# Loops for the gathers and for part of the slots, side work moved ahead

## The reference

```
hx: 272 tokens x 1024, normalized
scores of 8 heads x 2 halves against 128 keys each; the 16 best pairs per head
expert = 128 * index_a + index_b          # 8 heads x 16 = 128 experts per token, of 16384
gate   = softmax over the 16 of a head
act    = gelu(hx . peer_u[expert])        # one dot of 1024 per token and expert
y      = sum over the 128 of gate * act * peer_v[expert]
```

## Time and profile before

| | us |
|---|---|
| median of 3 runs | 2488.28 (2478.59 to 2488.97) |
| the profiled execution | 2487.36, span 2485.6 |
| PE busy | 1982.1 (80%) |
| DVE busy | 1413.1 (57%) |
| POOL busy | 1027.1 (41%), 528 + 528 gathers |
| ACT busy | 576.7 (23%) |

### The profile page before, as it was taken

How to read it: one execution, slowest core, us unless ns; L and a number is a source line. 1 busy time by engine, 2 the same in 40 slices (tenths; PEclk the granted TensorE clock), 3 DMA queues, 4 the chain that set the end, 5 groups by cost and what they waited for, 6 DMA issues and landing times.

```text
span 2485.6 us, 21257 instructions
## 1 busy us (share of the span) xinstructions
PE 1982.1 (80%) x6918; PEld 1101.4 (44%) x6918; DVE 1413.1 (57%) x3068; ACT 576.7 (23%) x1204; POOL 1027.1 (41%) x1063
## 2 busy tenths in 40 slices
PE   6756767767898789768877887688877799897998
PEld 3641222222333335423344463243322297676996
DVE  0138788755344554694455447855555455555884
ACT  1111100100112431011134211111100134453663
POOL 0025656766444454464444545656666400000000
PEclk9888989999998889999988899999999899998999
DMA  3257989999889789989966899999999744353653
GB/s 146 85 168 309 371 314 367 369 368 356 320 301 345 272 285 393 348 305 357 396 235 234 329 385 346 343 370 409 396 364 368 284 144 154 111 153 103 187 182 122
DMA packets 194843, 707.96 MB, mean 285 GB/s; under 512 B 21784, under 2 KB 23072, under 8 KB 194480
## 3 DMA queue, kind: packets, MB, share of 16 engines
q0 software_dynamic: 152064, 553.72, 59.6%
q1 hardware_dynamic: 40960, 150.65, 17.9%
q10 hardware_dynamic: 1712, 2.24, 0.3%
HBM read 704.81 MB, written 1.06 MB: 284 GB/s over the span
## 4 chain that ended last, share of the span: by engine, by line
PE 54%; DVE 17%; issue 10%; DMA 7%; POOL 6%; ACT 3%; another core or an unknown queue 1%; ACTq 0%; SPq 0%; DVEq 0%; POOLq 0%
PE ps L494 22%; PE ps L652 15%; DMA a<-in_peer_u,eidx 7%; PE ps L411 5%; PE ps L426 5%; DVE a L1435 4%; POOL a L349 3%; POOL a L344 3%; DVE diag L1444 1%; DVE a L1369 1%; PE ps L444 1%; PE ps L397 1%; PE ps L598 1%; DVE a L1375 1%
## 5 line engine op out<-in xcount | busy, mean ns | idle before, releaser
L494 PE MATMUL ps<-a,diag 128*128 128x512 f32 (+1 forms) x2112 | 1091.9, 657 | 356.2 <-DVE diag L1444 237.2
L494 PEld LDWEIGHTS ps<-a,diag 128*128 128x128 f32 (+1 forms) x2112 | 402.9, 203 | 994.2 <-issue 623.0
L1435 DVE SCALAR_TENSOR_TENSOR a<-a,ps 128x1024 f32<-128x1024 f32 x512 | 622.3, 1216 | 347.3 <-DMA a<-in_peer_u,eidx 289.3
L344 POOL DMA_INDIRECT a<-in_peer_u,eidx x528 | 522.5, 990 | 636.7 <-DVE a L1435 303.4
L349 POOL DMA_INDIRECT a<-in_peer_v,eidx x528 | 503.8, 954 | 303.3 <-issue 133.3
L652 PE MATMUL ps<-a_r 128*128 128x256 f32 (+1 forms) x1648 | 393.8, 332 | 19.9 <-DVE a_r L1583 7.3
L932 ACT ACTIVATE gel<-dots 128x1 f32<-128x1 f32 x528 | 101.1, 201 | 1076.6 <-DVE a L1435 637.9
L652 PEld LDWEIGHTS ps<-a_r 128*128 128x128 f32 x1648 | 279.6, 192 | 52.3 <-DVE a_r L1583 8.1
L1577 DVE TENSOR_TENSOR ring_r<-wring,a_r 128x1024 fp32r<-128x1024 f32 x142 | 173.3, 1222 | 139.8 <-ACT a_r L1091 139.7
L1444 DVE TENSOR_SCALAR diag<-cstc,gel,a 128x128 f32<-128x128 f32 (+1 forms) x528 | 186.1, 354 | 104.0 <-issue 38.9
L1091 ACT ACTIVATE a_r<-wring 128x1024 fp32r<-128x1024 f32 x142 | 149.4, 1053 | 82.3 <-PE ps L652 82.2
(11 more groups left out here) (218 smaller groups left out, 1299.1 us busy)
## 6 DMA issues: line engine op xcount, KB each, us to landing
wring<-in_units SPq DMA_DIRECT2D x270, 512.0 KB
a<-in_peer_u,eidx POOLq DMA_INDIRECT x528
a<-in_peer_v,eidx POOLq DMA_INDIRECT x528
cs2c<-in_cs SPq DMA_DIRECT2D x1, 1792.0 KB
a<-in_poolm SPq DMA_DIRECT2D x1, 1632.0 KB, 9.2
h<-in_xin SPq DMA_DIRECT2D x2, 512.0 KB, 4.2
bcF<-in_bc_rows SPq DMA_DIRECT2D x2, 512.0 KB, 9.3
a<-in_mem SPq DMA_DIRECT2D x1, 1024.0 KB, 4.9
```

Source lines behind the costliest of these rows:

```text
L344: g.indirect_dma_start(ug[:, n % NU, :], None, peer_u, bass.IndirectOffsetOnAxis(ap=eidx[:, t, k:k + 1], axis=0))\
L494: last = nc.tensor.matmul(ps[0:P, 6 + j, :], diag[:, k % 4, 0:P], vg[:, k % NV, j * 512:(j + 1) * 512], start=False, stop=False)
L1435: v.scalar_tensor_tensor(ug[:, n % NU, :], ug[:, n % NU, :], 1.0, hnm if t == 2 else ps2(4), ALU.mult, ALU.mult, accum_out=dots[:, k % 8:k ...
```

## The change

- POOL's gathers of the four big tiles are in loops (`g.Fori`) of 32 slots a turn. In a loop the number n is a register. Before every 16 slots POOL copies 16 columns of `eidx` into a new tile `ixc` of two halves and waits for the copy. The waits for `dot` and `vsum` stand apart from the gathers, as each is followed by an increment of a new semaphore (`u_go`, `v_go`) that nothing waits for; the two are built as one instruction. The 16 meta slots and the first tile's two halves stay as they were in order: the first tile has two loops of two turns.
- PE's sums of the first tile are a loop of four turns (`sums_loop`).
- DVE and ACT do slots 96 to 127 of the first tile in a loop of one turn, PE, ACT and DVE slots 64 to 127 of the last tile in a loop of two turns (`slots_loop`, `gelu_loop`, `sums_loop`). Buffer numbers come from the slot's place in the turn, the values waited for from registers.
- In `SIDE`, `flip` goes from 56 to 54 and `first` from 112 to 60; a new entry `end` = 64 is where the loops begin.

```diff
...
                                           "in_z", "br", "out", "up", "down"]
-SIDE = dict(mem=3, memT=6, mem_k=9, mem_v=22, trev=36, n2=42, n2T=46, x=49, flip=56, first=112)
+SIDE = dict(mem=3, memT=6, mem_k=9, mem_v=22, trev=36, n2=42, n2T=46, x=49, flip=54, first=60, end=64)
...
         ti = sb("ti", [128, 256], u32)
         bp = sb("bp", [128, 128], u32)
         pab = sb("pab", [128, 2, 128], u32)
+        ixc = sb("ixc", [128, 2, 16], u32)
         eidx = sb("eidx", [128, 3, 128], u32)
         dots = sb("dots", [128, 8])
         gel = sb("gel", [128, 8])
...
             g.memset(ss[:, :], 1.0).then_inc(S("zeroed"), 1)
             g.memset(hsum[:, :], 1.0).then_inc(S("zeroed"), 1)
-            def slot(t, k, n):
-                if n >= NU:
-                    g.wait_ge(S("dot"), n + 1 - NU)
-                g.indirect_dma_start(ug[:, n % NU, :], None, peer_u,
-                                     bass.IndirectOffsetOnAxis(ap=eidx[:, t, k:k + 1], axis=0))\
-                    .then_inc(S(f"u{n % NU}"), 16)
-                if n >= NV:
-                    g.wait_ge(S("vsum"), n + 1 - NV)
-                g.indirect_dma_start(vg[:, n % NV, :], None, peer_v,
-                                     bass.IndirectOffsetOnAxis(ap=eidx[:, t, k:k + 1], axis=0))\
-                    .then_inc(S(f"v{n % NV}"), 16)
+            n_idx = [0]
+            def indices(half, src):
+                g.tensor_copy(ixc[:, half, :], src).then_inc(S("ixc"), 1)
+            def slot(l, k, n, half, col):
+                if not isinstance(n, int) or n >= NU:
+                    g.wait_ge(S("dot"), n + (1 - NU))
+                    g.sem_inc(S("u_go"), 1)
+                g.indirect_dma_start(ug[:, k % NU, :], None, peer_u,
+                                     bass.IndirectOffsetOnAxis(ap=ixc[:, half, col:col + 1], axis=0))\
+                    .then_inc(S(f"u{k % NU}"), 16)
+                if not isinstance(n, int) or n >= NV:
+                    g.wait_ge(S("vsum"), n + (1 - NV))
+                    g.sem_inc(S("v_go"), 1)
+                g.indirect_dma_start(vg[:, k % NV, :], None, peer_v,
+                                     bass.IndirectOffsetOnAxis(ap=ixc[:, half, col:col + 1], axis=0))\
+                    .then_inc(S(f"v{k % NV}"), 16)
             for l in range(2):
                 for t, base in gathers(l):
                     g.wait_ge(S("eidx"), tk_number(l, t))
-                    for k in range(16 if t == 2 else SLOTS):
-                        if (l, t, k) == (0, 0, SLOTS // 2):
-                            g.wait_ge(S("eidx"), tk_number(0, 0, 1))
-                        slot(t, k, base + k)
+                    if t == 2:
+                        indices(1, eidx[:, t, 0:16])
+                        n_idx[0] += 1
+                        g.wait_ge(S("ixc"), n_idx[0])
+                        for k in range(16):
+                            slot(l, k, base + k, 1, k)
+                        continue
+                    done = n_idx[0]
+                    turns = SLOTS // GB
+                    for part, (i0, i1) in enumerate([(0, turns // 2), (turns // 2, turns)] if (l, t) == (0, 0)
+                                                    else [(0, turns)]):
+                        if part:
+                            g.wait_ge(S("eidx"), tk_number(l, t, part))
+                        with g.Fori(i0, i1) as i:
+                            for half in range(2):
+                                indices(half, eidx[:, t, ds(i * GB + 16 * half, 16)])
+                                g.wait_ge(S("ixc"), 2 * i + (done + half + 1))
+                                for kk in range(16):
+                                    k = 16 * half + kk
+                                    slot(l, k, GB * i + (base + k), half, kk)
+                    n_idx[0] += 2 * (SLOTS // GB)
         @block.tensor
         def _(pe):
...
                 last.then_inc(S("y_pe"), 1)
                 owe("y", m, 6, 7)
+            def sums_loop(base, start=0):
+                with pe.Fori(start // GB, SLOTS // GB) as i:
+                    for k in range(GB):
+                        sums_slot(128, k, GB * i + (base + k), 16 * (GB // NV) * i + 16 * ((base + k) // NV + 1))
             def beside(base):
                 return Beside(lambda k: sums_slot(128, k, base + k, 16 * ((base + k) // NV + 1)), LAG)
...
                 sums_slot(META, k, m_base + k, 16 * ((m_base + k) // NV + 1))
             sums_end(2, 1)
             sums_begin(128)
-            first = beside(a_base)
-            first.to(SLOTS + LAG)
+            sums_loop(a_base)
             sums_end(0, 2)
             def front(i, bg):
...
                                         start=True, stop=True)
             last.then_inc(S("flip_pe"), 1)
             owe("bias", 1, 0, 1, 2, 3)
-            bg.to(SLOTS + LAG)
+            bg.to(SIDE["end"] + LAG)
+            sums_loop(b_base, SIDE["end"])
             sums_end(1, 5)
             owe("dot", 16 + 4 * SLOTS, 4, 5)
...
                 nc.scalar.activation(gel[:, k % 8:k % 8 + 1], dots[:, k % 8:k % 8 + 1], ACT.Gelu)\
                     .then_inc(S("gelu"), 1)
+            def gelu_loop(base, start=0):
+                with act.Fori(start // GB, SLOTS // GB) as i:
+                    for k in range(GB):
+                        gelu(k, GB * i + (base + k))
             def beside(base):
                 return Beside(lambda k: gelu(k, base + k))
...
             gate_exps(0, 0, 1)
             first.to(TOPK_B)
             gate_exps(0, 1)
-            first.to(SLOTS)
+            first.to(STRAIGHT)
+            gelu_loop(a_base, STRAIGHT)
             x_row(1)
             y_out(0, 2)
...
             bg.to(SIDE["first"])
             w_high(SPLIT0)
             w_high(SPLIT0 + 1)
-            bg.to(SLOTS)
+            bg.to(SIDE["end"])
+            gelu_loop(b_base, SIDE["end"])
             y_out(1, 5)
...
                 link(v.reciprocal(gs[:, h0:h0 + H], gm[:, h0:h0 + H]))
                 link(v.tensor_tensor(G3, G3, gs[:, h0:h0 + H].unsqueeze(2).to_broadcast([128, H, 16]), ALU.mult))
-            def dot(t, k, n):
-                dve.wait_ge(S(f"u{n % NU}"), 16 * (n // NU + 1))
-                if t < 2 and k == 0:
+            def dot(t, k, n, ufill=None):
+                dve.wait_ge(S(f"u{k % NU}"), 16 * (n // NU + 1) if ufill is None else ufill)
+                if t < 2 and isinstance(n, int) and n % SLOTS == 16:
                     dve.wait_ge(S("x_row"), (n - 16) // SLOTS + 1)
-                v.scalar_tensor_tensor(ug[:, n % NU, :], ug[:, n % NU, :], 1.0, hnm if t == 2 else ps2(4),
+                v.scalar_tensor_tensor(ug[:, k % NU, :], ug[:, k % NU, :], 1.0, hnm if t == 2 else ps2(4),
                                        ALU.mult, ALU.mult, accum_out=dots[:, k % 8:k % 8 + 1]).then_inc(S("dot"), 1)
             def coef(t, k, n, gate):
                 unit_mat, W = (cc("sel", 16), 16) if t == 2 else (ident, 128)
                 dve.wait_ge(S("gelu"), n + 1)
-                if n >= 4:
+                if not isinstance(n, int) or n >= 4:
                     dve.wait_ge(S("vsum"), n - 3)
                 v.tensor_scalar(diag[:, k % 4, 0:W], unit_mat, gel[:, k % 8:k % 8 + 1], gate,
                                 ALU.mult, ALU.mult).then_inc(S("diag"), 1)
...
             def flush(t, base, n):
                 for k in (n - 2, n - 1):
                     coef(t, k, base + k, gates[t][:, k:k + 1])
+            def slots_loop(t, base, start=0):
+                with dve.Fori(start // GB, SLOTS // GB) as i:
+                    for k in range(GB):
+                        dot(t, k, GB * i + (base + k), 16 * (GB // NU) * i + 16 * ((base + k) // NU + 1))
+                        if k >= 2:
+                            coef(t, k - 2, GB * i + (base + k - 2), gates[t][:, ds(GB * i + (k - 2), 1)])
+                    for k in (GB - 2, GB - 1):
+                        coef(t, k, GB * i + (base + k), gates[t][:, ds(GB * i + k, 1)])
             norm("f0", [0, 1, 2], 3, gain=bcF[:, :])
...
             topk(0, 0, lambda n: bg.to(min(TOPK_A, TOPK_A * n / HALF_GATE_AT)), part=1)
             dve.wait_ge(S("sc0_ev"), 3)
             topk(0, 1, lambda n: bg.to(min(STRAIGHT, TOPK_A + (TOPK_B - TOPK_A) * n / GATE_AT)))
-            bg.to(SLOTS)
-            flush(0, a_base, SLOTS)
+            bg.to(STRAIGHT)
+            flush(0, a_base, STRAIGHT)
+            slots_loop(0, a_base, STRAIGHT)
             def heads_norm(tag, tiles):
...
             bg.to(SIDE["first"] + 1)
             w_low(SPLIT0)
             w_low(SPLIT0 + 1)
-            bg.to(SLOTS)
-            flush(1, b_base, SLOTS)
+            bg.to(SIDE["end"])
+            flush(1, b_base, SIDE["end"])
+            slots_loop(1, b_base, SIDE["end"])
             dve.wait_ge(S("vsum"), 16 + 4 * SLOTS)
```

## The result

The changed kernel takes 2502.47 us (median of 5 runs, 2500.34 to 2510.94), the kernel before 2485.21 us (5 runs, the three shown above and two more). The ratio is 1.0081, 95% interval 1.0056 to 1.0106: 20 us slower, by the medians 17. It was measured twice more in the experiments, 1.0082 (1.0063 to 1.0102) and 1.0080 (1.0064 to 1.0096).

A forecast was written before the change was run, and what follows sets the result against it. Row arrival by DMA was taken to bound the first and last tile, with POOL hardly faster. POOL's terms 25 + 19 + 21 = 65 us, times 0.27, gave 18 us: 2487.4 + 18 = 2505 us, range 2484 to 2562.

The forecast's parts named there:

- The bound: In the first and last tile slots come as fast as rows arrive; POOL, hardly faster, has 0.08 us margin per slot.
- Term 1: On POOL, 33 index copies for the loops at 0.75 us each, between 0.4 and 1.15: 25 us.
- Term 2: On POOL, separate waits ahead of gathers, charged only where POOL waits: 234 gathers at 0.08 us, 19 us.
- Term 3: On POOL, 11 jumps back in the loops, each charged an instruction fetch of 1.9 us: 21 us.
- Terms 4 and 5: Loops of PE, DVE and ACT (0 to 3 us) and the last tile's moved side work (below 2 us): both 0.
- The share of 0.27: Part of POOL's added 65 us reaching the kernel's end, from POOL's 27% of the last tile's chain: 18 us.
- B: Nothing arrives: POOL's additions go under DMA backlog, jumps find code, copies disappear in waits; 0 to 6 us; chance 0.28.
- C: On POOL, all 1044 waits and 608 additions cost 0.08 us each, uncovered: 69 us more, 2556 us; chance 0.18.
- D: Faster: more evenly spaced gathers keep PE's array from pausing, 15 us less, 2472 us; chance 0.09.

The follow-up runs named there:

- the first set's chip: The chip of the first four follow-up runs, where the kernel before takes 2426.3 us; on the other sets' chips it takes 2485.6 and 2484.9 us.
- experiment 7: The kernel before, written out, with each gather's wait in a separate incrementing instruction and two further increments behind it, 2088 more in all: ratio 1.0092.

## Why the prediction came out, and where it was wrong

The time was right, 2502.5 us for 2505 forecast, and so was its direction. The way there was right in its frame (POOL is what the change loads, the dense tiles are where it shows, the rest costs nothing) and wrong in what each of its three terms costs and in the share that arrives; these errors cancelled. That the time came within 3 us is luck.

- **The bound.** Right as to the place, the first and the last tile: the two grew by 14.2 us and the middle ones shrank by 2.2, while the span grew by 12.9.
- **Term 1, the copies, 25 us of POOL.** The size on POOL was right in the changed kernel: 0.81 us each for 0.75 taken, 27 us in all. What was wrong is what they cost. Alone they cost 1.0007, twice, with intervals that hold 1; they were alone only with 0.18 us each, but on top of the separate waits, where the gather behind them is late as in the changed kernel, they didn't show either (1.0061 and 1.0062, in different sets).
- **Term 2, the separate waits, 19 us of POOL.** The step that failed, by the size of its term. "I charge it only where POOL arrives too early and waits" was right: back-to-back gaps stayed 0.30 us in every kernel, even with 2088 further instructions. The price of 0.08 us was not: 0.54 us (0.81 - 0.27). The 0.39 us against 0.30 in rows 3 and 4 was read as the cost of a semaphore; it is only how much later than the earliest moment that dot's signal came. What the trace did show was that a waiting gather starts 0.27 us after its releaser, and the question to ask was what of its preparation had been done by then. My reading: when the gather carries the wait, all of it had; when an instruction ahead waits, the gather's own handling begins afterwards. The records bear it out: the increment passes its wait 0.03 or 0.04 us after the dot's end, and the gather starts 0.76 us behind the increment. In the kernel before 166 gathers of the four tiles stand 0.5 us or more behind their predecessor, those that waited for indices left out; at 0.54 us each that is 90 us of later starts, not 19.
- **Term 3, the jumps, 21 us.** Nothing. A jump back takes 0.05 us on POOL's sequencer (the eleven records of 53 ns; the five of 40 ns are the loops' ends), ahead of a copy that starts on time, and q14 moved 49 packets for 50 before. The fetch that was charged didn't come: by the Trainium skill, "Runtime: NRT & Kernel Launch", section on instruction fetch mechanics, a taken branch has to fetch before execution goes on where its target lies outside the two-page window. No run here shows a stall of that kind, with bodies of 11 KB by the prediction's estimate. Whether POOL's loops cost a little beyond the copies and waits (1.0076 to 1.0061, intervals overlapping) stays open.
- **Terms 4 and 5.** 0 and 0, and measured 0.9994 (on the first set's chip) and 1.0000.
- **The share of 0.27.** It held for the sum only because both factors were off. 90 us of waits give 15 us by the ratio of 1.0062, a share of 0.17 over all tiles. By tiles: the two dense ones have 45 late gathers, 24 us, and grew by 16, two thirds; the middle ones have 121, 65 us, and grew by 2.5. One share for the whole kernel mixes the two. Nor is it one share for all chips: the 108 gathers of U on the first set's chip make 58 us of later starts in the dense tiles, and the kernel grew by 2.4 us.
- **The rivals.** B was right for the copies and the jumps. C's mechanism, waits that aren't covered, didn't happen where POOL works back to back; the part of it that did is term 2. D didn't happen: the granted clock is 0.927 before and after.

Why 27 us of copies vanish and 90 us of late starts don't is read from the traces above and not tested by a run of its own. A copy falls, as most gathers do, where the DMA engines have rows to move (2% and 4% idle behind it in the table). On the slower chips a late start falls where POOL has waited and the engines are running out (15% idle behind it already in the kernel before), so the next rows come later by what the start is late.

## What to carry to other kernels

A wait that a DMA on GpSimd carries itself costs 0.27 us from its releaser; the same wait in an instruction ahead makes it 0.81 us, and each further small instruction between adds 0.08. It costs nothing while the engine has work before it, and little where the DMA engines still have rows to move (58 us of later starts gave 0.1% on the first set's chip). So it must be counted per start at which the DMA engines have run out, and not per start after a wait. Rolling loops up was free on PE, DVE and ACT here; on GpSimd the greater part of the price was not the loop but that its gathers no longer carried their waits.

## What the runs showed of the hardware

- POOL's sequencer runs ahead of the gathers: it took a jump back 5.9 us before the copy behind the jump, with four gathers still to run. Six instructions per pair of gathers more (experiment 7) leave the 0.30 us between gathers as they were.
- The records of such instructions mislead: an increment is recorded with 17 ns, a register addition with 32 ns, while a further increment costs 0.08 us on the path.
- The same kernel took 2426 us on one chip and 2485 on two others, with the difference in the gather stages (389 GB/s in the first tile against 358). The separate waits are worth 0.1% on one and 0.6% on another.
- The semaphore events differ with the chip too. In all kept traces of the first set 529 events of `vsum` and 529 of `dot` are recorded for 528 slots; in those of the slower chips 375 to 408 and 315 to 368. There some events of `vsum` come in bursts. In the kernel before, the last four groups of sums ahead of 1876 us end, as modelled, at 1866.6, 1869.4, 1871.9 and 1874.4, and four events are recorded between 1876.21 and 1876.38; the gather of V that had waited 4.18 us starts at 1876.46, and the DMA engines then have the hole shown above. Bursts of three or four events stand 12 times in the dense tiles of the kernel before, 8 to 16 times in the other traces of the slower chips, and never in the first set's. No run tried what makes them.
